# Two-layer encoder on one core: the next layer's modulation rows computed on VectorE during the output projection of layer 0

## The reference, as far as it matters

```
ca = silu(c)
for l in range(2):
    mod = ca @ w_ada[l] + b_ada[l]
    sh1, sc1, gt1, sh2, sc2, gt2 = split(mod, 6)
    h = rms_norm(x, g_norm1[l]) * (1 + sc1) + sh1
    proj = h @ w_in[l]
    mix = concat(four head groups of proj) @ w_out[l]
    x = x + gt1 * mix
    h2 = rms_norm(x, g_norm2[l]) * (1 + sc2) + sh2
    x = x + gt2 * hier_moe(h2)
return rms_norm(x, g_final)
```

## Time and profile before

| | |
|---|---|
| median of 3 runs | 1861.46 us (1860.07 to 1866.36) |
| profiled execution, its own time | 1866.84 us |
| its span | 1865.0 us |
| TensorE matmuls busy | 1581.0 us, 85% |
| VectorE busy | 693.6 us, 37% |
| ScalarE busy | 436.8 us, 23% |
| GpSimd busy | 210.7 us, 11% |
| DMA | 527.56 MB, mean 283 GB/s |

### The profile page before, as it was taken

One profiled execution on the slowest core, in us unless ns is written; L12 is line 12 of the kernel. 1 busy time (PEld: TensorE's weight loads), 2 busy tenths in 40 slices (PEclk: granted clock), 3 DMA queues, 4 the chain that ended last, 5 costly groups with the idle time before them and its releaser, 6 DMA issues.

```text
span 1865.0 us, 22498 instructions
## 1 busy us (share of the span) xinstructions
PE 1581.0 (85%) x7432; PEld 765.3 (41%) x7432; DVE 693.6 (37%) x1413; ACT 436.8 (23%) x989; POOL 210.7 (11%) x215
## 2 busy tenths in 40 slices
PE   4999898998887998888779998999699877877783
PEld 2455555553333333333235554455333333333331
DVE  1577466442222122222157836733422212222124
ACT  2111466211211111111121116641111211111111
POOL 2000022111111101111020002101111111111000
PEclk7999989999999999999979998999799999999997
DMA  9616332159999999999882443310899999999994
GB/s 354 221 68 211 127 111 83 40 217 403 395 402 407 414 400 405 414 410 416 344 286 91 137 179 111 111 46 38 314 377 364 401 412 410 410 416 406 402 401 163
DMA packets 119384, 527.56 MB, mean 283 GB/s; under 512 B 17040, under 2 KB 23280, under 8 KB 70416
## 3 DMA queue, kind: packets, MB, share of 16 engines
q1 hardware_dynamic: 101808, 493.66, 67.6%
q0 software_dynamic: 13104, 24.51, 4.3%
q10 hardware_dynamic: 4400, 8.46, 1.2%
HBM read 521.06 MB, written 23.86 MB: 292 GB/s over the span
## 4 chain that ended last, share of the span: by engine, by line
PE 59%; DMA 26%; DVE 7%; issue 3%; ACT 3%; SPq 1%; DVEq 0%; ACTq 0%; POOLq 0%
DMA ring<-in_w_exp_up 24%; PE ps L1299 21%; PE ps L963 17%; PE ps L1164 6%; PE ps L1297 3%; PE ps L1106 2%; PE ps L1120 2%; PE ps L989 2%; PE ps L1146 2%; DMA ring<-in_w_ada 1%; PE ps L1325 1%; PE ps L978 1%; DVE arena L662 1%; ACT arena L1586 1%; PE ps L1133 1%
## 5 line engine op out<-in xcount | busy, mean ns | idle before, releaser
L1299 PE MATMUL ps<-ring,arena 128*64 128x512 f32 x2864 | 654.4, 609 | 128.4 <-DMA ring<-in_w_exp_up 63.2
L1299 PEld LDWEIGHTS ps<-ring,arena 128*64 128x64 f32 x2864 | 220.8, 140 | 518.2 <-issue 509.1
L963 PE MATMUL ps<-ring,hT 128*128 128x512 f32 (+1 forms) x768 | 257.0, 489 | 2.3 <-ACT tmp L1486 2.1
L662 DVE TENSOR_TENSOR arena<-ps,arena 64x512 f32<-64x512 f32 (+1 forms) x64 | 44.3, 692 | 502.4 <-ACT arena L1580 434.2
L1580 ACT ACTIVATE arena<-ps 128x512 f32<-128x512 f32 x64 | 38.2, 597 | 807.5 <-PE ps L1299 754.1
L963 PEld LDWEIGHTS ps<-ring,hT 128*128 128x128 f32 x768 | 144.9, 191 | 103.1 <-issue 91.3
L928 POOL DMA_INDIRECT yexp_d<-arena,masks x64 | 59.3, 926 | 877.7 <-DVE arena L672 877.7
L670 DVE TENSOR_TENSOR arena<-ps,gate 64x512 f32<-64x512 f32 (+1 forms) x64 | 43.7, 682 | 281.9 <-PE ps L1299 261.4
L1164 PE MATMUL ps<-ring,hT 128*128 128x512 f32 x256 | 112.5, 595 | 0.0
L1572 ACT ACTIVATE arena<-ps,modc 128x128 f32<-128x128 f32 x256 | 96.5, 457 | 33.2 <-PE ps L1276 30.8
L1717 DVE SCALAR_TENSOR_TENSOR probsT<-z,convw,probsT 128x512 f32<-128x512 f32 x120 | 90.0, 751 | 3.9
(11 more groups left out here) (220 smaller groups left out, 1423.0 us busy)
## 6 DMA issues: line engine op xcount, KB each, us to landing
ring<-in_w_exp_down SPq DMA_DIRECT2D x128, 1024.0 KB, 23.8
ring<-in_w_exp_gate SPq DMA_DIRECT2D x124, 1024.0 KB, 21.2
ring<-in_w_exp_up SPq DMA_DIRECT2D x124, 1024.0 KB, 23.6
ring<-in_w_ada SPq DMA_DIRECT2D x24, 2048.0 KB, 9.8
ring<-in_w_in SPq DMA_DIRECT2D x8, 2048.0 KB, 21.2
ring<-in_w_out SPq DMA_DIRECT2D x4, 2048.0 KB, 8.4
ring<-in_w_in SPq DMA_DIRECT2D x6, 1024.0 KB, 8.7
xn_d<-arena ACTq DMA_DIRECT2D x8, 512.0 KB, 2.9
```

What stands on the lines that cost most here:

```text
L963: last = pe.matmul(out, lhs(k), rhs(k), start=(k == 0), stop=(k == n - 1))
L1299: last = [pe.matmul(outs[c][HALF * c:HALF * c + HALF, :], lhs(k)[:, 0:HALF], rhs(c, k), start=(k == 0), stop=(k == n - 1), tile_position=( ...
```

## The change

The four `ADA_NEXT` units are no longer multiplied on TensorE. VectorE multiplies each with `row_product`, the former body of `early_product`, into `next_sum` (free parts of `arena`), counted by `next_ready`. Units 0 and 1 are multiplied ahead of the first output tile, unit 2 ahead of tile 1's scaling and unit 3 ahead of tile 2's. TensorE only adds up the partitions in `mod_next`, 8 matmuls of one column for each unit, behind the ranks (units 0 and 1) and behind the further lists (2 and 3). SyncE's waits for these four slots are for `next_ready`; in layer 0 the first expert units are issued in the order down 0, gate 1, up 1, down 1, gate 0, up 0. In both layers all six are issued ahead of the wait for the last logits. The wait for the last modulation row ahead of `probsT` is gone.

```diff
--- before.py
+++ after.py
@@ -223,7 +223,6 @@
         for n, (m, u) in enumerate(ADA_NEXT[l]):
             if n == NORM1_UNITS // 2:
                 take((l, "rank"), 5)
-            take((m, "ada", u), "mm")
         if not ADA_NEXT[l]:
             take((l, "rank"), 5)
         for n, (m, u) in enumerate(ADA_NEXT[l]):
@@ -289,6 +288,7 @@
                 tuple(probs[:, 2 * k:2 * k + 2, :].rearrange("p a s -> p (a s)") for k in range(2)),
                 (probsT[:, :, :, :].rearrange("p a t q -> p (a t q)"), tmp[:, :, :].rearrange("p a s -> p (a s)"))]
         rT = sb("rT", [P, 2, P])
+        next_sum = [arena[:, c:c + 512] for c in (5120, 5632, 8192, 8704)]
         early_sum = [arena[:, 4096 + 512 * i:4096 + 512 * i + 512] for i in range(4)]
         cst = sb("cst", [P, NCONST])
         C = {k: cst[:, C_AT[k]:C_AT[k] + w] for k, w in CONSTS.items()}
@@ -363,7 +363,7 @@
         dve_chain, pool_chain = sem("dve_chain"), sem("pool_chain")
         ada_in = sem("ada_in")
         mod_ready = sem("mod_ready")
-        early_ready = sem("early_sum_ready")
+        early_ready, next_ready = sem("early_sum_ready"), sem("next_sum_ready")
         sq_summed = sem("sq_summed")
         sq_ready = sem("sq_ready")
         sqA_ready = sem("sqA_ready")
@@ -630,8 +630,6 @@
             link(dve.tensor_tensor(gates[:, 1, :], gates[:, 0, :], rt[:, dv:dv + TT], ALU.mult))
             for m, u in ADA_NEXT[l][:2]:
                 mod_out(m, u)
-            for n, (m, u) in enumerate(ADA_NEXT[l][2:]):
-                ada_turned(m, u, n)
             link(slot_lists((l, "more_lists"), NE, P))
             dve.sem_inc(more_ready, 1)
             for m, u in ADA_NEXT[l][2:]:
@@ -714,7 +712,9 @@
                 if POS[unit] >= SLOTS:
                     old = AT[POS[unit] - SLOTS]
                     key = last_use(old)
-                    if key:
+                    if ORDER[old][0] == "ada" and ORDER[old][1] and ORDER[old][2] < NORM1_UNITS:
+                        sp.wait_ge(next_ready, ORDER[old][2] + 1)
+                    elif key:
                         await_filled(sp, key)
                     else:
                         _, lo, e3 = ORDER[old]
@@ -785,20 +785,16 @@
                     for h in range(2):
                         load_half(unit, h, w3[c][0, j])
 
-                for n in range(4):
+                for n in [2, 3, 4, 5, 0, 1] if ADA_NEXT[l] else range(6):
                     first_expert_unit(n)
                 await_filled(sp, (l, "last_logits"))
                 for h in range(2):
                     sp.dma_start(hT[:, 4 * h:4 * h + 4, :].rearrange("p k n -> p (k n)"), w3[0][1, 0][:, 2048 * h:2048 * h + 2048])\
                         .then_inc(ahead_in[0][h], 16)
-                for n in range(4, 6):
-                    first_expert_unit(n)
                 sp.wait_ge(slots_ready, 2 * l + 2)
                 if not ADA_NEXT[l]:
                     sp.wait_ge(xg_in[0], 16 * (l * HE + 1))
                 sp.dma_start(probs[:, :, :].rearrange("p k n -> p (k n)"), w3[1][1, 0][:, 0:2048]).then_inc(ahead_in[1][0], 16)
-                for m, u in ADA_NEXT[l][-1:]:
-                    await_filled(sp, (m, "mod", u))
                 sp.dma_start(probsT[:, :, :, :].rearrange("p k a n -> p (k a n)"), w3[1][1, 0][:, 2048:3072]).then_inc(ahead_in[1][1], 16)
                 sp.dma_start(tmp[:, :, :].rearrange("p k n -> p (k n)"), w3[1][1, 0][:, 3072:4096]).then_inc(ahead_in[1][1], 16)
                 for n in range(3 * AHEAD + 2, 18):
@@ -1223,8 +1219,16 @@
                         logits(t - 2)
 
                 half = NORM1_UNITS // 2
-                for m, u in ADA_NEXT[l][:half]:
-                    ada(m, u)
+
+                def mod_next(m, u):
+
+                    key, p0 = (m, "mod", u), HALF * (u % 2)
+                    pe.wait_ge(next_ready, u + 1)
+                    await_free(pe, key)
+                    for k in range(KD):
+                        last = pe.matmul(bank(key)[p0:p0 + HALF, k:k + 1], next_sum[u][:, k:512:KD], C["ones"][:, 0:1],
+                                         start=True, stop=True, tile_position=(0, p0))
+                    fills(last, key)
 
                 key = (l, "rank")
                 pe.wait_ge(hots_ready, l + 1)
@@ -1232,8 +1236,8 @@
                 n = TT * NE + NE
                 pe.matmul(bank(key)[:, 0:n], C["ones"], sums.rearrange("p t e -> p (t e)"), start=True, stop=False)
                 fills(pe.matmul(bank(key)[:, 0:n], C["before"], hots5, start=False, stop=True), key)
-                for n, (m, u) in enumerate(ADA_NEXT[l][:half]):
-                    mod(m, u, n)
+                for m, u in ADA_NEXT[l][:half]:
+                    mod_next(m, u)
 
                 key = (l, "list_parts")
                 pe.wait_ge(slots_ready, 2 * l + 1)
@@ -1246,14 +1250,12 @@
                 key = (l, "lists")
                 await_free(pe, key)
                 fills(pe.matmul(bank(key)[:, 0:NE], list_parts, C["fold32"], start=True, stop=True), key)
-                for m, u in ADA_NEXT[l][half:]:
-                    ada(m, u)
                 key = (l, "more_lists")
                 pe.wait_ge(slots_ready, 2 * l + 2)
                 await_free(pe, key)
                 fills(product(bank(key)[:, NE:P], lambda n: slot_hot[:, n, :], lambda n: slot_val[:, n, NE:P], n=2 * TT), key)
-                for n, (m, u) in enumerate(ADA_NEXT[l][half:]):
-                    mod(m, u, n)
+                for m, u in ADA_NEXT[l][half:]:
+                    mod_next(m, u)
 
 
                 def bank_e(b):
@@ -1552,8 +1554,6 @@
                         act.dma_start(xn2_d[l].rearrange("(t p) d -> t p d", p=P)[t - 1], xs[:, t - 1, :]).then_inc(xn_out, 16)
                     if t < TT:
                         squares(l, 2, [t])
-                for n, (m, u) in enumerate(ADA_NEXT[l][:2]):
-                    ada_out(m, u, n)
                 for n in range(2):
                     act.wait_ge(rin_ready, 2 * l + n + 1)
                     r = rt[:, 0:16] if n == 0 else rt[:, 16:20]
@@ -1756,17 +1756,23 @@
                         await_drained(dve, (l, "conv_in", 2 * f + 1))
                     dve.wait_ge(table_in, 16 * N_TABLES * (l + 1))
 
+                def next_product(m, u):
+
+                    row_product(UNIT["ada", m, u], next_sum[u], next_ready)
+
                 def early_product(i):
 
-                    unit = UNIT[("ada",) + ADA_EARLY[l][i]]
+                    row_product(UNIT[("ada",) + ADA_EARLY[l][i]], early_sum[i], early_ready)
+
+                def row_product(unit, acc, ready):
+
                     await_unit(dve, unit)
-                    acc = early_sum[i]
                     link(dve.tensor_scalar(acc, slot(unit)[:, 0, :], csil[:, 0:1], None, ALU.mult))
                     for k in range(1, KD):
                         ins = dve.scalar_tensor_tensor(acc, slot(unit)[:, k, :], csil[:, k:k + 1], acc, ALU.mult, ALU.add)
                         if k < KD - 1:
                             link(ins)
-                    ins.then_inc(early_ready, 1)
+                    ins.then_inc(ready, 1)
 
                 for gi_, g in enumerate(GROUPS):
                     for t in range(TT):
@@ -1911,7 +1917,12 @@
                 dve.tensor_tensor(router, wr[:, :, :], columns(3), ALU.mult).then_inc(router_ready, 1)
                 link(dve.tensor_tensor(shifted, wr[:, :, :], columns(2), ALU.mult))
                 dve.tensor_reduce(shift_sum, shifted.rearrange("p k e -> p e k"), AX_X, ALU.add).then_inc(router_ready, 1)
+                for m, u in ADA_NEXT[l][:2]:
+                    next_product(m, u)
                 for t in range(TT + 1):
+                    if t in (1, 2):
+                        for m, u in ADA_NEXT[l][t + 1:t + 2]:
+                            next_product(m, u)
                     if t < TT:
                         for n in range(2):
                             key = (l, "out", t, n)
```

## The result

The changed kernel takes 1878.53 us in the median of 4 runs (1877.2 to 1882.59), the kernel before 1862.18 in the same comparison. The ratio is 1.0089 with a 95% interval of 1.0065 to 1.0113: slower by 12 to 21 us. A second comparison, with 5 runs against 17, gave 1875.76 and a ratio of 1.0057 (1.0043 to 1.0071), so 8 to 13 us. The profiled execution took 1877.65 us for a span of 1875.7, 10.7 over the span before. The forecast was 1875, with +13.9 for the change.

What follows compares the result with a forecast made beforehand. Layer 0's end was taken as set by bytes left to load and stream pauses. First expert 429.3 + 10.3 + 2 = 441.6, refill 448.0, stream 471.2 + 8: last landing 927.2, +13.9, so 1875 us; range 1864 to 1883.

Steps and rivals of the forecast that it cites:

- Stop of TensorE: Layer 0 output stage: TensorE stands still 8.2 us ahead of tile 0's transposes, behind two VectorE products and GpSimd's additions.
- Clock behind it: After TensorE's idle time at tile 0, restarting at the 1.2 GHz level costs +2.1 us (0 to 3).
- Products 2 and 3: VectorE's third and fourth products, behind the scaling of output tiles, are covered; without cover each would cost up to 6 us.
- rival C: VectorE is late for output tiles 1 and 2 too, adding 6 to 12 us, about 1884 us; chance 0.1.
- Routing: Layer 0, last logits to first expert: row products go, one-column matmuls come; +2 us, ends -1 and +5.
- First refill: Layer 0's first ring refill comes 6.4 us behind the first expert, at 448.0.
- Stream: Layer 0, first refill to last landing: 191.8 MB at 407 GB/s, 471.2 us, plus 8 us loss.
- loss with the full ring: Behind layer 0's first refill, refills wait for TensorE to empty a half slot: 8 us, ends 2 and 12.
- gain of 7.7 us: Layer 0's stream: all eight units in before the first expert, 3.1 MB more than before, saves 7.7 us.
- Rival A: Early loads come through: TensorE's stop under 2 us, ring loss 2, last landing 4.9 us earlier; chance 0.06.
- Rival B: No change: TensorE stops without clock loss, routing is free, ring loses 2; +3.8 us, 1865.3 us; chance 0.08.
- Rival D: SyncE, held by a wait, doesn't issue down 0 before 389.8; about +20 us, 1881 us; chance 0.03.

Runs made afterwards that it cites:

- second profile of the changed kernel: The changed kernel measured once more, nothing altered: 1875.76 us, ratio 1.0057 to the kernel before.
- both repairs: Changed kernel with products 0 and 1 in VectorE's idle stretches late in attention and one-column groups ahead of the ranks: 1861.87 us, ratio 0.9979 to the kernel before.

## Why the prediction was right

The direction, the place and the size of the stop came as forecast, and so did what follows from it up to the first expert. In the stream the total was right and its two parts were not.

- *Stop of TensorE*: forecast 8.2 us, released by GpSimd; measured 7.69 in the profile, and 7.68 or 7.69 in the four other profiles with two products ahead. VectorE reached the tile at 370.30 (forecast 370.4).
- *Clock behind it*: forecast +2.1; measured 0.93 on the transposes and 0.90 on the next tile, 1.8. In the second profile of the changed kernel that tile took 16.04 us, so there 3.1, just over the 0 to 3 that I gave; in the three other profiles with the same stop it took 14.38, 14.44 and 14.82, so 1.4 to 1.9. The granted clock was 0.50, as forecast.
- *Products 2 and 3*: covered, as forecast. There is no further idle time ahead of the transposes of tiles 1 and 2 (390.01 and 406.43), and rival C falls.
- *Routing*: forecast +2; measured 27.96 against 25.64 us, +2.3. The first expert was forecast for 441.6 and came at 441.59. Some of that accuracy is luck, as the terms deviate by 0.3 to 0.5 us in both directions.
- *Loads*: down 0 was forecast near 364 and went at 364.50, the last of the four near 394 and went at 393.56. The DMAs moved nothing in the last 4 us ahead of the first refill, as forecast.
- *First refill*: 5.6 us behind the first expert, not 6.4, 0.8 too many in the sum. In the second profile it is 6.35: the first expert's matmuls took 8.99 us in the one and 9.75 in the other.
- *Stream*: forecast 479.2 us, measured 478.0. The loss with the full ring was put at 8 us for the first 142 us, and 382 GB/s there makes (1 - 382/407) x 141.5 = 8.7; but the rest of the stretch ran at 411 GB/s, and over the whole of it 192.3 MB in 478.0 us are 5.5 us more than at 407. The gain of 7.7 us was too large as well. At the first refill the kernel before had 14.35 MB of weights in and the changed one 16.8, which is 6.0 us at 407 GB/s; I had counted at 434.5, and not at the refill. The two errors are of like size and cancel. That the total came within 1.2 us is in part luck.
- *Layer 1*: 482.9 us from first refill (1348.68) to last landing (1831.58), before 483.0: unchanged, and its two earlier loads are worth nothing, as forecast.

The sum of +13.9 stands against +11.7 at the last landing, +10.7 in the spans, +16.3 and +11.6 in the medians. It is 2.2 us over the trace: 0.8 from the refill, 1.2 from the stream, the rest from rounding; the stop's 0.5 too many is made up by the routing and by 0.3 us that this execution reached the stage later. Spans differ from landings, as the stretch from the last landing of layer 0 to the first refill of layer 1 takes from 421.0 to 428.6 us in the ten profiles (424.7 before, 423.5 after), which I did not trace to a cause. I can't settle from these runs which of the two ratios is nearer the truth.

Rival A (the early loads come through) falls twice: in the changed kernel for want of its condition, and in the kernels without the stop in itself, since with the stop gone the early order is still worth nothing. Of the 5.7 us of DMA time that the early order saves there, 1.4 come through in the stream, and nothing in the median. Its argument, the idle stretch of the stream from 322 to 390, was true and without consequence: the stretch between the last output tile and the first refill is long enough to load nearly all that fits. Rival B would have needed the clock to hold and the routing to be free, and neither was so. Rival D falls with SyncE's timeline.

What I had not seen is how little was wrong with the change. The 24 us of VectorE's products cost nothing once two of them stand inside waits of 8.9 and 6.3 us, and with the one-column groups out of the path too the kernel is 2 to 6 us faster than before. TensorE is rid of 11.9 us of row products (5.33 and 6.54) in the routing, but the rows show that the first of the two groups was not in the way. In the kernel before the ranks began behind it at 409.40, and with both repairs, whose output stage runs at the same times, at 409.46:

```profile
409.40 0.54 PE L1233 MATMUL ps<-probs,cst 128*128 128x160 f32 x2
```

The second group did delay the lookup, which now begins at 419.84 in place of 421.81, and of these 2.0 us its low clock takes 1.7 back (3.73 us in place of 2.02). The other part is that no modulation rows stand between the lookup and the tokens' transposes any more, for whose bank TensorE waited 2.35 us in the kernel before. Which of the two is worth how much was not tried apart.

## What to carry to other kernels

An engine that is idle for two thirds of a stage is not free at each place of it: ask which instruction of the other engines waits for the next one in its list, and put added work into a gap that the timeline shows, as long as the work. Before moving loads forward, look at when the buffers are full in any case and when the first of them is emptied. If the first is earlier than the second, the loads can't gain anything, and what delays the emptying costs its full length. If a little is missing at that point, the gain can be less than its DMA time: here 1.4 us for 5.7. An idle stretch of the DMAs that lies ahead of such a point is no reserve.

## What the runs showed of the hardware

- The stream is slower while the ring is full: 382 to 385 GB/s in the 142 us behind the first refill with eight units in, 388 with 7.7, 398 to 401 with 6.0 to 6.9 units in, 407 over a whole stage that never pauses. That this comes from refills which have to wait for a half slot was argued from the order of the loads, not tested by itself.
- One-column matmuls of 128 x 64 weights took the same time at either clock: 3.55 us for 32 rows of the trace at a granted clock of 1.00 (410.14, before) and of 0.50 (420.81 to 424, after); a lookup with 96 columns took 2.02 and 3.73 us.
- The clock fell behind the last logits whatever came next. In the kernel before, where the logits end at 403.7 and row products of 512 columns follow at 404.13, it was 0.54 from 404 to 406 and back at 1.00 from 408 to 410. With both repairs, where the three groups of one column follow at 403.56, it was 0.53 from 404 to 406 and stayed at 0.50, though TensorE worked on them without a gap until 408.6; the ranks behind them took 0.90 us and the lookup 3.73, as after an idle wait. These are stretches (length, busy time of TensorE, of its weight loads and so on, then granted clock, DMA share, GB/s), the first two of the kernel before, the others with both repairs:

```profile
404.00:406.00 2.00, 1.87 (x12) 0.71 (x16) 1.75 (x13) 0.00 (x0) 0.00 (x0) 0.54 1.00 401
408.00:410.00 2.00, 2.00 (x20) 0.84 (x12) 1.54 (x6) 0.88 (x2) 1.58 (x2) 1.00 0.69 131
```
```profile
404.00:406.00 2.00, 2.00 (x22) 2.00 (x22) 1.76 (x13) 0.22 (x1) 0.00 (x0) 0.53 1.00 401
406.00:408.00 2.00, 2.00 (x23) 2.00 (x22) 1.86 (x17) 0.68 (x2) 0.26 (x1) 0.50 1.06 446
```
